# Chunked attention heads run on across tiles: one slot of other work per score group, an own bank for the short group, moves by half tiles

## The chip, the cores and the metric

One core of one Trainium2 chip runs the whole program. The metric is device time in microseconds (us) of one execution; lower is better. A profile of one execution gives the times of single instructions.

## The reference

A residual block over 4096 positions of width 1024, with two parallel groups. `h = rms_norm(x)` and `proj = h @ w_in` give a pooling mixer (value, gate) and eight attention heads of width 64 (q, k, v, gate). Each chunk of 64 positions attends to itself and the eight chunks before it:

```python
s = einsum('bqhd,bkhd->bhqk', qb, kb) * scale + bias      # clipped relative positions
s = where(valid, s, MASK_VALUE)
p = softmax(s, axis=-1)
y_attn = einsum('bhqk,bkhd->bqhd', p, vb) * silu(attn_g)
x = x + concatenate([y_pool, y_attn]) @ w_out
return rms_norm(x, final_norm_gain)
```

## The kernel before

Every operand of a matmul is split into a high and a low fp16 part, and the input projection is a seven-product scheme on blocks. The program has three phases, each written as one list of instructions for each engine, with semaphores between them; the order written out is the order in which each engine works.

**First phase** (`h_phase_*`): 16 pairs of 128-row blocks are normalised, split and stored in `h_dram`, with the value and gate columns. x comes through two buffers, one load ahead. At pair 5 SP (the engine that issues the transfers) sends the relative-bias rows, written out per query and per key for all heads, from DRAM to DRAM. **Second phase** (`q_phase_*`): the pooling branch and its half of the output projection, whose sum goes to `r_dram`.

**Third phase** (`a_phase_*`): 16 tiles of 256 queries. For each of eight heads TensorE issues:
- `maxima` (two, for the two blocks of 128 queries): scores by query in the double bank `wide`; VectorE's `maximum` adds the bias and takes the row maximum. They run two heads ahead.
- `max_rows`: the maxima as a row in bank `tra`; ScalarE's `max_row` copies it into the query operand, so that the next scores come out with the maximum taken off. One head ahead.
- `scores`: up to three groups of columns by key (512, 512 and 256), turn by turn in the two banks `sta[n % 2]`; VectorE's `add_bias` works on the second; ScalarE's `exponential` writes `p32` (two buffers) and rounds it to `p_h`; GpSimd's `p_lo` makes the low part.
- `values`, one head behind: both parts with V, into `pva`; VectorE's `attend` normalises and gates into `y`.

Between them stand pieces of other work: the key and query projection of the next tile (`kq_half`, 14 products in 28 halves; products take turns in `bankx` and `banky`, with `kq_take` on VectorE and copies on ScalarE; `kq_hi` and `kq_lo` round the finished operand), and the output projection of an earlier tile (`output`, four parts in two halves, `residual` on VectorE). `KQ_SLOTS` says how many halves each head takes; heads 6 and 7 take halves of the output instead.

Between two tiles stands `boundary(t)`: the rest of the output of tile t-2, the last head's `values`, the transposes of `y` (`branch_transposes`, in `tra` and `wide`, rounded by `branch_hi` and `branch_lo`), and the first two heads' maxima with eight product halves among them. The new keys and queries go by twelve transfers within SBUF (`move_k`, `move_q`, 128 KB each) to their operand places, sent once the tile before has all its scores. Then follow V (`load_v`), the gates, the residual, and seven loads of the projection's operand two tiles on (`load_hop3`), all on SP's one queue.

Of the kernel before, what the change touches and what calls it, by code (L numbers as in the profile page):

```python
# [20 lines left out]
P = 128  # L21
# [78 lines left out]
def build(nc, x, norm_gain, w_in, pool_w, pool_scale, rel_fwd, rel_rev, w_out, final_gain, out):  # L100
# [13 lines left out]
    with ctx:  # L114
# [3 lines left out]
        def sem(name):  # L118
# [21 lines left out]
        Z = sb("stages", [P, 38400 // 4], F32)  # L140
# [60 lines left out]
        p32 = view(Z, 18432, (2, 512), F32)  # L201
# [6 lines left out]
        names = """ident0 ident_ready id16 consts log_ready inv_ready ones_ready gain_loaded pw_loaded small_loaded  # L208
# [3 lines left out]
            ext_done ext_stored bias_stored over""".split()  # L212
# [280 lines left out]
        def h_phase_dve(dve):  # L493
# [120 lines left out]
            def bias_rows():  # L614
# [3 lines left out]
                nc.vector.tensor_copy(ident16[:, :], ident[:, :]).then_inc(H["id16"], 1)  # L618
# [166 lines left out]
        def h_phase_sp(sp):  # L785
# [33 lines left out]

            load_x(0)  # L820
# [24 lines left out]
            for p in range(1, PAIRS):  # L845
# [25 lines left out]
        names = """psc_done over mm p1_done u_done c11_done tanh_done z_done step_done y_done yh_done yl_done op_mm r_done  # L871
# [384 lines left out]
        def q_phase_pool(pool):  # L1256
# [30 lines left out]
            pool.wait_ge(H["bias_stored"], 32)  # L1287
# [9 lines left out]
        def q_phase_sp(sp):  # L1297
# [58 lines left out]
            load_gate(sp, 0)  # L1356
            load_bias(sp)
            move_k(sp, 0)
            for s in range(PRODUCTS):
                load_hop3(sp, 1, s)  # L1360
            for b in range(PBLK):
                n = PBLK * (PTILES - 1) + b
                store_res(n)
                if b < 2:
                    load_res(n + 2)
                if b == 1:
                    move_q(sp, 0)
            for s in range(2):
                sp.wait_ge(r_stored[s], 16 * 2 * PTILES)
            sp.nop().then_inc(Q["over"], 1)  # L1370

        names = """moved_k moved_q kq_mm kq_p kq_u nat_hi nat_lo v_loaded gate_loaded k_ones mask_rows bias_q_loaded
# [5 lines left out]
        hop3_loaded = [sem(f"a_hop3_loaded{s}") for s in range(PRODUCTS)]  # L1378
        res_loaded = [sem(f"a_res_loaded{s}") for s in range(2)]
# [46 lines left out]

        KQ_PRODUCT = (0, 1, 2, 3, 4, 6, 5)
        KQ_TAKES = {1: 0, 2: 1, 3: 2, 5: 3, 6: 4}


        KQ_BEFORE = 8
        KQ_SLOTS = ((2, 2), (2, 1), (2, 1), (2, 1), (2, 1), (2, 2), (0, 0), (0, 0))
        K_HI_AT, Q_HI_AT = (2, 0), (6, 0)

        def slot(h, i):

# [711 lines left out]
```

## Time and profile before

| | before |
|---|---|
| time, median of 3 runs | 1805.46 us (1803.0 to 1809.53) |
| time of the profiled execution | 1807.35 us |
| its span, first to last instruction | 1805.6 us |
| TensorE busy | 1644.2 us (91%) |
| VectorE busy | 1068.5 us (59%) |
| ScalarE busy | 843.5 us (47%) |
| GpSimd busy | 708.4 us (39%) |
| mean granted TensorE clock | 0.984 |

The busy time of an engine is the union of its instructions' times. TensorE's matmuls overlap one another, so that its busy time is no measure of how fast it could go. Idle time of an engine is put down to the instruction that it waited for.

### The profile page before, as it was taken

The numbers are of one execution on the slowest core, as the hardware profiler recorded it, in microseconds if no ns is written. First come the engines' busy times: TensorE is split into PE (matmuls) and PEld (weight loads), VectorE is DVE, ScalarE is ACT, GpSimd is POOL, SyncE is SP. The second block draws the span as 40 slices with busy tenths as digits, with TensorE's granted clock in tenths as the row PEclk, the third lists the DMA queues.
The fourth block names the chain that finished last, engine by engine and source line by source line (L and its number), as shares of the span: only waits on it lengthen the run. The fifth ranks groups of instructions, "written<-read, shape, count | busy, mean of one in ns | idle before, by whom it ended". The sixth has DMA issues, their size and how long they took to land. (4 is left out here: it accounts for less than half of the span.)

```text
span 1805.6 us, 43913 instructions
## 1 busy us (share of the span) xinstructions
PE 1644.2 (91%) x17920; PEld 1220.5 (68%) x17920; DVE 1068.5 (59%) x2188; ACT 843.5 (47%) x1580; POOL 708.4 (39%) x734
## 2 busy tenths in 40 slices
PE   5999699999999999999879999999999999999977
PEld 2554345568667676777567787778777787778854
DVE  7767477747456556544355565556655565556654
ACT  5554455422112111111145766567565765667565
POOL 3534345311112121001324644465545654456544
PEclk8999899999999999999989999999999999999999
DMA  5655574462542453244743342442334332442332
GB/s 205 209 204 200 196 247 170 170 251 72 186 164 83 163 187 129 83 159 166 218 147 101 99 131 79 136 131 106 102 106 148 112 125 72 136 148 90 107 94 83
DMA packets 111231, 257.84 MB, mean 143 GB/s; under 512 B 11928, under 2 KB 24744, under 8 KB 108984
## 3 DMA queue, kind: packets, MB, share of 16 engines
q1 hardware_dynamic: 109992, 253.73, 42.0%
q8 instruction: 143, 2.34, 0.5%
q0 software_dynamic: 1040, 1.31, 0.4%
q14 instruction: 56, 0.46, 0.1%
HBM read 151.33 MB, written 83.48 MB: 130 GB/s over the span
## 5 line engine op out<-in xcount | busy, mean ns | idle before, releaser
L2029 POOL TENSOR_TENSOR stages<-stages 128x512 f16<-128x512 f32 (+1 forms) x368 | 379.3, 1046 | 445.3 <-ACT stages L1814 445.1
L1489 PE MATMUL bank<-middle,weights 128*128 128x128 f16 x1792 | 315.0, 220 | 14.0 <-DVE middle L1526 13.1
L1492 PE MATMUL bank<-middle,weights 128*128 128x128 f16 x1792 | 314.6, 220 | 0.0
L1491 PE MATMUL bank<-middle,weights 128*128 128x128 f16 x1792 | 314.5, 220 | 0.0
L1808 ACT ACTIVATE stages<-bank,log_ps 128x512 f32<-128x512 f32 (+1 forms) x368 | 222.0, 603 | 163.9 <-POOL stages L2029 93.4
L1899 DVE CUSTOM_DVE_ANT_0 stages<-bank,stages 128x640 bf16<-128x640 f32 (+4 forms) x256 | 200.0, 781 | 158.2 <-PE bank L1647 157.9
L975 PE MATMUL bank<-middle 128*128 128x256 f16 x784 | 215.7, 275 | 7.5 <-DVE stages L1103 7.5
L977 PE MATMUL bank<-middle 128*128 128x256 f16 x784 | 215.7, 275 | 0.0
L978 PE MATMUL bank<-middle 128*128 128x256 f16 x784 | 215.6, 275 | 0.0
L1677 PE MATMUL bank<-middle 128*128 128x128 f16 (+1 forms) x840 | 169.4, 244 | 46.5 <-ACT stages L1808 41.9
L1814 ACT ACTIVATE stages<-stages 128x512 f16<-128x512 f32 (+1 forms) x368 | 203.5, 553 | 11.7
L288 PE MATMUL bank<-weights,middle 128*128 128x512 f16 x448 | 172.5, 385 | 25.9 <-DVE stages L584 15.9
L1489 PEld LDWEIGHTS bank<-middle,weights 128*128 128x128 f16 x1792 | 175.9, 98 | 17.5 <-DVE middle L1526 15.9
L1623 PE MATMUL bank<-entry,stages 128*128 128x512 f16 x768 | 181.1, 379 | 1.6 <-DVE stages L1876 1.0
L998 PE MATMUL bank<-entry,stages 128*128 128x512 f16 x768 | 171.6, 380 | 11.4 <-DVE entry L1195 11.4
L1491 PEld LDWEIGHTS bank<-middle,weights 128*128 128x128 f16 x1792 | 176.1, 98 | 0.4
L1492 PEld LDWEIGHTS bank<-middle,weights 128*128 128x128 f16 x1792 | 175.8, 98 | 0.0
L290 PE MATMUL bank<-weights,middle 128*128 128x512 f16 x448 | 172.2, 384 | 0.0
L291 PE MATMUL bank<-weights,middle 128*128 128x512 f16 x448 | 171.9, 384 | 0.0
L1262 POOL TENSOR_TENSOR stages<-stages 128x512 f16<-128x512 f32 x32 | 39.4, 1230 | 282.1 <-ACT stages L1051 282.1
L998 PEld LDWEIGHTS bank<-entry,stages 128*128 128x128 f16 x768 | 74.3, 98 | 101.2 <-DVE entry L1195 17.3
L1680 PE MATMUL bank<-middle 65*128 65x256 f16 x616 | 130.3, 242 | 0.0
(147 smaller groups left out, 3544.3 us busy)
## 6 DMA issues: line engine op xcount, KB each, us to landing
entry<-in_x SPq DMA_DIRECT2D x64, 512.0 KB, 3.6
h_ops<-middle SPq DMA_DIRECT2D x16, 1792.0 KB, 6.1
middle<-h_ops SPq DMA_DIRECT2D x112, 256.0 KB, 5.1
middle<-h_ops SPq DMA_DIRECT2D x49, 512.0 KB, 6.9
middle<-middle SPq DMA_DIRECT2D x192, 128.0 KB, 2.3
residual<-entry SPq DMA_DIRECT2D x32, 512.0 KB, 2.8
entry<-residual SPq DMA_DIRECT2D x30, 512.0 KB, 4.1
out<-entry SPq DMA_DIRECT2D x30, 512.0 KB, 2.9
```

The lines of the kernel that those rows point to most:

```text
L975: nc.tensor.matmul(bank, wh, hop[:, :, s, 0, kt, :], start=(kt == 0 and s < 4), stop=False, skip_group_check=True)
L977: nc.tensor.matmul(bank, wh, hop[:, :, s, 1, kt, :], start=False, stop=False, skip_group_check=True)
L978: mm = nc.tensor.matmul(bank, wl, hop[:, :, s, 0, kt, :], start=False, stop=(kt == 3), skip_group_check=True)
L998: mm = nc.tensor.matmul(op[n2], part, w[:, kt, n2 * 512:(n2 + 1) * 512], start=(kt == 0 and w is wot_h and part is yh), stop=(kt == NKT - ...
L1489: nc.tensor.matmul(dst, wh, hop3[:, o, 0, kt, :], start=(kt == 0 and s < 2 and pair == 0), stop=False, skip_group_check=True)
L1491: nc.tensor.matmul(dst, wh, hop3[:, o, 1, kt, :], start=False, stop=False, skip_group_check=True)
L1492: mm = nc.tensor.matmul(dst, wl, hop3[:, o, 0, kt, :], start=False, stop=(kt == 3), skip_group_check=True)
L1623: mm = nc.tensor.matmul(bank[:, :], yh, w, start=(m == 0), stop=(m == 11))
L1808: nc.scalar.activation(p32[:, s, a:b], sta[s][:, a:b], ACT.Exp, bias=log_ps[:, 0:1]).then_inc(A["exp_done"], 1)
L1814: nc.scalar.activation(p_h[:, h % 2, c + a:c + b], p32[:, s, a:b], ACT.Copy).then_inc(A["ph_done"], 1)
L1899: nc.vector.tensor_tensor_reduce(junk2[:, c:640], wide[:, c:640], bias_q[:, h, c:640], 1.0, -3e38, ALU.add, ALU.max, m16[:, h % 2, j:j + 1 ...
L2029: nc.gpsimd.tensor_tensor(p_l[:, h % 2, c + a:c + b], p32[:, s, a:b], p_h[:, h % 2, c + a:c + b], ALU.subtract).then_inc(A["pl_done"], 1)
```

## The change

The part between tiles is gone. `ahead(t, h, n)` counts heads across tiles, so maxima and row maxima of the next tile are issued in the last heads of this one, and the last head's values in the first head of the next. Each head has three slots (`SLOTS`), one behind each score group; slots 0 to 13 take one whole product each, slots 15 to 22 one half of the output of the tile before; slots 14 and 23 are empty. The products' banks alternate over both operands. Each score group has its own bank and its own `p32` buffer; the short one lies in the second half of `pva` and waits until the head before is normalised. The transposes go in two rounds of four, by halves of the heads, at the ends of the first two heads of the next tile, both in `tra`. Keys, queries and gates are moved by halves of the heads, the first half while the tile before still works on its second. In the last tile the output of the tile before stands in slots 7 to 14, and the first halves of its own output in slots 17 to 20. In the first phase the bias rows are sent in four parts, two heads at each of the pairs 5 to 8. Some semaphores that nobody waits for are gone.

```diff
...
-p32 = view(Z, 18432, (2, 512), F32)
+p32 = [view(Z, 18432, (512,), F32), view(Z, 20480, (512,), F32), view(Z, 38144, (2 * P,), F32)]
...
+    def store_bias(h):
+        if h == 0:
+            sp.wait_ge(H["ext_stored"], 16)
+        for r, (dst, width) in enumerate(((bq_dram, 640), (bk_dram, 256))):
+            sp.dma_start(dst[h:h + 2], bass.AP(rel_dram.tensor, (r * HEADS + h) * EXT + P - 1,
+                                       [[EXT, 2], [-1, P], [1, width]])).then_inc(H["bias_stored"], 16)
...
-        if p == BIAS_AT + 2:
-            sp.wait_ge(H["ext_stored"], 16)
-            for r, (dst, width) in enumerate(((bq_dram, 640), (bk_dram, 256))):
-                sp.dma_start(dst, bass.AP(rel_dram.tensor, r * HEADS * EXT + P - 1,
-                                          [[EXT, HEADS], [-1, P], [1, width]])).then_inc(H["bias_stored"], 16)
+        if 0 <= p - BIAS_AT - 2 < HEADS // 2:
+            store_bias(2 * (p - BIAS_AT - 2))
...
+SLOTS = 3
+K_HI_HEAD, Q_HI_HEAD = 2, 4
+HALF = HEADS // 2
+def kq_slot(t, h, a):
+    x = SLOTS * h + a
+    return divmod(x, PRODUCTS) if t < LAST and x < 2 * PRODUCTS else None
+def output_slot(t, h, a):
+    x = SLOTS * h + a
     if t == LAST:
-        return ((t - 1, h - 4, i),) if h >= 4 else ()
-    return ((t - 1, h - 6, i),) if t > 0 and h >= 6 else ()
+        if 7 <= x < 15:
+            return t - 1, (x - 7) // 2, (x - 7) % 2
+        return (t, x - 17, 0) if 17 <= x < 21 else None
+    return (t - 1, (x - 15) // 2, (x - 15) % 2) if t > 0 and 15 <= x < 23 else None
+def round_at(t, h):
+    if t > 0 and h < 2:
+        return t - 1, h
+    return (t, 0) if t == LAST and h == HALF else None
+def squares_at(t, h):
+    if t == LAST:
+        return {3: ((t - 1, 0),), 5: ((t - 1, 1),)}.get(h, ())
+    return {6: ((t - 1, 0),), 7: ((t - 1, 1),)}.get(h, ()) if t > 0 else ()
+def finish_at(t, h):
+    found = ((t - 2, 1),) if t > 1 and h == 0 else ()
+    if t == LAST:
+        return {4: ((t - 1, 0),), 6: ((t - 1, 1),)}.get(h, found)
+    return ((t - 1, 0),) if t > 0 and h == 7 else found
...
-def kq_bank(s):
-    bank = (bankx, banky, bankx, banky, bankx, banky, bankx)[s]
+def kq_bank(w, s):
+    bank = (bankx, banky)[(w + s) % 2]
     at = (0, 0, AT, AT, 0, AT, AT)[s]
     return bank[:, at:at + AT]
...
-    dst = kq_bank(s)[:, pair * P:(pair + 1) * P]
+    dst = kq_bank(w, s)[:, pair * P:(pair + 1) * P]
...
-def load_gate(sp, t):
-    at_least(sp, A["ya_done"], 2 * HEADS * t)
+def load_gate(sp, t, half):
+    at_least(sp, A["ya_done"], 2 * HEADS * t if half else 2 * HEADS * t - 2 * HALF)
+    cols = slice(half * AT, (half + 1) * AT)
     for j in range(2):
-        sp.dma_start(gate[:, j, :], z_dram[2 * t + j]).then_inc(A["gate_loaded"], 16)
+        sp.dma_start(gate[:, j, cols], z_dram[2 * t + j, :, cols]).then_inc(gate_loaded[half], 16)
...
+def scored(t, half):
+    return seq(t - 1, HEADS if half else HALF, 0)
+def move_q(sp, t, half):
     sp.wait_ge(A["nat_lo"], 2 * t + 2)
     if t > 0:
-        sp.wait_ge(A["st_mm"], seq(t - 1, HEADS, 0))
+        sp.wait_ge(A["st_mm"], scored(t, half))
+    h2 = slice(2 * half, 2 * half + 2)
     for o in range(2):
-        half = slice(o * DH, (o + 1) * DH)
-        move(sp, qs[0:DH, o, :, :], nat[half, 1, 0, :, :], "moved_q")
-        move(sp, qs[DH:P, o, :, :], nat[half, 1, 1, :, :], "moved_q")
-        move(sp, qm[0:DH, o, :, :], nat[half, 1, 0, :, :], "moved_q")
...
+def before(t, h, g):
+    at, head = (t, h - 1) if h > 0 else (t - 1, HEADS - 1)
+    if at < 0:
+        return 0
+    have = [x for x, _ in groups(at)]
+    return seq(at, head, have.index(g)) + 1 if g in have else 0
...
+def score_bank(g):
+    return (sta[0][:, :], sta[1][:, :], pva[:, 2 * P:4 * P])[g]
...
+def out_bank(t, i):
+    if t == LAST:
+        return (bankx[:, :], banky[:, :], wide[:, 0:512], wide[:, 512:1024])[i]
+    return (bankx[:, :], banky[:, :])[i % 2]
...
+            if t == LAST and i >= 2:
+                pe.wait_ge(A["max_done"], 2 * HEADS * ATILES)
+            else:
+                at_least(pe, A["out_done"], 4 * t + i - 1)
             if i < 2 and t < LAST:
                 pe.wait_ge(A["kq_u"], 5 * min(2 * t + 6, 2 * ATILES))
+        elif t == LAST:
+            pe.wait_ge(A["ytl_done"], 2 * t + 2)
         for m in range(6 * half, 6 * half + 6):
             kt, p = m // 3, m % 3
             yh = (yT_l if p == 2 else yT_h)[:, kt, j * P:(j + 1) * P]
             w = (wob_l if p == 1 else wob_h)[:, kt, n2 * 512:(n2 + 1) * 512]
-            mm = nc.tensor.matmul(bank[:, :], yh, w, start=(m == 0), stop=(m == 11))
+            mm = nc.tensor.matmul(out_bank(t, i), yh, w, start=(m == 0), stop=(m == 11))
         if half == 1:
...
         n = 2 * HEADS * t + 2 * h + j
         if n > 0:
             pe.wait_ge(A["max_done"], n)
...
+        if h >= 2 and round_at(t, h - 2):
+            of, r = round_at(t, h - 2)
+            pe.wait_ge(A["ytl_done"], 2 * of + r + 1)
         for j in range(2):
             mm = nc.tensor.matmul(tra[:, j * P:(j + 1) * P], m16[:, h % 2, j:j + 1].to_broadcast([P, P]),
                                   ident16[:, :], start=True, stop=True)
...
             pe.wait_ge(A["mrow_done"], HEADS * t + h + 1)
+        if g == 2:
...
+    def branch_transposes(t, r, rows):
+        pe.wait_ge(A["ya_done"], 2 * (HEADS * t + HALF * (r + 1)))
+        pe.wait_ge(A["mrow_done"], rows)
+        for q in range(4):
+            kt = 2 * r + q // 2
+            mm = nc.tensor.transpose(tra[:, q * P:(q + 1) * P], y[:, q % 2, kt * P:(kt + 1) * P], ident[:, :])
         mm.then_inc(A["yt_mm"], 1)
...
+    def other(t, h, a):
+        if kq_slot(t, h, a):
+            x = SLOTS * h + a
+            kq_half(pe, t + 1, 2 * x)
+            kq_half(pe, t + 1, 2 * x + 1)
+        if output_slot(t, h, a):
+            output(*output_slot(t, h, a))
+    def head(t, h):
+        scores(t, h, 0)
+        other(t, h, 0)
+        t2, h2 = ahead(t, h, 2)
+        if t2 < ATILES:
+            maxima(t2, h2, 0)
+        scores(t, h, 1)
+        t1, h1 = ahead(t, h, 1)
+        if t1 < ATILES:
+            max_rows(t1, h1)
+        other(t, h, 1)
+        if t > 0 or h > 0:
+            values(*ahead(t, h, -1))
+        if t2 < ATILES:
+            maxima(t2, h2, 1)
+        other(t, h, 2)
+        scores(t, h, 2)
+        if round_at(t, h):
+            of, r = round_at(t, h)
+            branch_transposes(of, r, HEADS * t + h + 2)
+    for j in range(2):
+        maxima(0, 0, j)
+    max_rows(0, 0)
+    for j in range(2):
+        maxima(0, 1, j)
+    for t in range(ATILES):
         for h in range(HEADS):
-            last = len(groups(t)) - 1
-            for k in range(2):
-                if k < last or (k == 0 and last == 0):
-                    scores(t, h, k)
-                if t < LAST:
-                    for x in slot(h, k):
-                        kq_half(pe, t + 1, x)
-                for at, i, half in output_slot(t, h, k):
-                    output(at, i, half)
-                if k == 0 and h + 1 < HEADS:
-                    max_rows(t, h + 1)
-                if h + 2 < HEADS:
-                    maxima(t, h + 2, k)
-            if last > 0:
-                scores(t, h, last)
-            if h > 0:
-                values(t, h - 1)
-    for t in range(ATILES):
-        boundary(t)
-        heads(t)
+            head(t, h)
     values(LAST, HEADS - 1)
-    for j in range(2):
-        branch_transposes(LAST, j)
+    branch_transposes(LAST, 1, HEADS * ATILES)
...
         if n == 0:
             act.wait_ge(Q["op_mm"], PBLK * PTILES)
...
+    def head(t, h):
+        exponential(t, h, 0)
+        other(t, h, 0)
+        exponential(t, h, 1)
+        t1, h1 = ahead(t, h, 1)
+        if t1 < ATILES:
+            max_row(t1, h1)
+        other(t, h, 1)
+        if t < LAST and h == K_HI_HEAD:
+            kq_hi(act, 2 * t + 2)
+        other(t, h, 2)
+        exponential(t, h, 2)
+        if t < LAST and h == Q_HI_HEAD:
+            kq_hi(act, 2 * t + 3)
+        if round_at(t, h):
+            branch_hi(*round_at(t, h))
+        for of, j in squares_at(t, h):
+            square(of, j)
+        if t == 0 and h < NKT:
+            wob_hi(h)
+    max_row(0, 0)
...
+    def branch_lo(t, r):
+        dve.wait_ge(A["yth_done"], 2 * t + r + 1)
         nc.vector.scalar_tensor_tensor(
-            out=yT_l[:, :, j * P:(j + 1) * P], in0=bank[:, 0:512].rearrange("p (k n) -> p k n", k=NKT),
...
+    def other(t, h, a):
+        if kq_slot(t, h, a):
+            w, s = kq_slot(t, h, a)
+            if s in KQ_TAKES:
+                kq_take(dve, 2 * t + 2 + w, KQ_TAKES[s])
+        if output_slot(t, h, a):
+            of, i, half = output_slot(t, h, a)
+            if half == 1:
+                residual(of, i)
+    def head(t, h):
+        other(t, h, 0)
+        t0, h0 = ahead(t, h, -1)
+        if t0 >= 0 and round_at(t0, h0):
+            branch_lo(*round_at(t0, h0))
+        t2, h2 = ahead(t, h, 2)
+        if t2 < ATILES:
+            maximum(t2, h2, 0)
+        add_bias(t, h)
+        other(t, h, 1)
+        if t > 0 or h > 0:
+            attend(t0, h0)
+        if t2 < ATILES:
+            maximum(t2, h2, 1)
+        other(t, h, 2)
+        for of, j in finish_at(t, h):
+            finish(of, j)
+        if t == 0 and h < NKT:
+            wob_lo(h)
...
@@ -2041,16 +2069,17 @@
     for t in range(ATILES):
         for h in range(HEADS):
-            p_lo(t, h)
-            if t > 1 and h in (1, 2):
-                rstd(t - 2, h - 1)
-            if t < LAST and h == K_HI_AT[0]:
-                kq_lo(pool, 2 * t + 2)
-            if t < LAST and h == Q_HI_AT[0]:
+            for k, (g, _) in enumerate(groups(t)):
+                p_lo(t, h, k)
+                if k == 0:
+                    for of, j in finish_at(t, h):
+                        rstd(of, j)
+                if g == BIASED and t < LAST and h == K_HI_HEAD:
...
-            load_gate(sp, t)
+            load_gate(sp, t, 1)
...
-            for j in range(2):
-                store(t - 2, j)
         if t > 0:
             for j in range(2):
                 load_residual(t - 1, j)
-        if t + 2 < ATILES:
-            for s in range(PRODUCTS):
-                load_hop3(sp, t + 2, s)
+        if t < LAST:
+            move_k(sp, t + 1, 0)
+            if t + 2 < ATILES:
+                for s in range(PRODUCTS):
+                    load_hop3(sp, t + 2, s)
+            load_gate(sp, t + 1, 0)
+            move_q(sp, t + 1, 0)
...
```

## Rows read from the trace of the kernel before

**Rows 1.** Windows, thirteen tiles: busy us and (instructions) per engine, clock, DMA share, GB/s
```profile
984.00:1734.00 750.00, 690.56 (x10714) 587.44 (x10713) 439.26 (x1066) 479.33 (x884) 401.15 (x390) 1.00 0.37 114
```

**Rows 2.** Waits of TensorE, 984 to 1734: total us, times, longest
```profile
PE bank L1677 <- ACT stages L1808: 37.4, 65, 1.3
PE bank L1489 <- DVE middle L1526: 10.5, 13, 0.8
PE bank L1647 <- DMA middle<-middle: 8.4, 10, 1.3
```

**Rows 3.** Timeline of TensorE in one head: start us, length us
```profile
1183.22 0.22 PE L1677 MATMUL bank<-middle 128*128 128x128 f16 x1
...
1183.67 0.22 PE L1489 MATMUL bank<-middle,weights 128*128 128x128 f16 x1
...
1184.34 0.44 PE L1647 MATMUL bank<-middle 128*128 128x128 f16 x4
1184.62 0.27 PE L1677 MATMUL bank<-middle 128*128 128x256 f16 x1
...
1184.84 0.19 PE L1705 MATMUL bank<-middle,stages 128*128 128x65 f16 x1
...
1185.71 0.19 PE L1707 MATMUL bank<-middle,stages 128*128 128x65 f16 x1
```

**Rows 4.** Timeline of three engines around the bias rows, 164 to 197
```profile
166.31 7.04 SPq L867 DMA_DIRECT2D bias_by_key<-rel_rows  x1
...
190.29 1.06 ACT L335 ACTIVATE entry<-entry 128x1024 bf16<-128x1024 f32 x1 [22.54 <-DMA entry<-in_x]
...
196.76 0.59 PE L288 MATMUL bank<-weights,middle 128*128 128x512 f16 x1 [15.87 <-DVE stages L584]
```

**Rows 5.** Lines of three engines, 1214 to 1445: busy us, mean ns, idle before
```profile
L1899 DVE CUSTOM_DVE_ANT_0 stages<-bank,stages 128x640 bf16<-128x640 f32 x64 | 52.7, 823 | 40.9 <-PE bank L1647 40.8
L1913 DVE TENSOR_TENSOR bank<-bank,stages 128x512 f32<-128x512 f32 x32 | 22.2, 695 | 17.0 <-PE bank L1680 17.0
L1526 DVE SCALAR_TENSOR_TENSOR middle<-bank,middle 128x256 f32<-128x256 f32 x40 | 16.9, 422 | 7.0 <-PE bank L1492 5.7 <-issue 1.2
L1931 DVE SCALAR_TENSOR_TENSOR middle<-bank,rc,middle 128x64 f32<-128x64 f32 x64 | 15.2, 280 | 1.1
...
L1924 DVE RECIPROCAL rc<-bank 128x2 f32<-128x2 f32 x32 | 5.4, 170 | 8.0 <-PE bank L1707 7.9
L1876 DVE SCALAR_TENSOR_TENSOR stages<-bank,stages 128x512 f16<-128x512 f32 x8 | 5.2, 686 | 1.5 <-ACT stages L1784 1.5
...
L1808 ACT ACTIVATE stages<-bank,log_ps 128x512 f32<-128x512 f32 x64 | 43.8, 685 | 25.7 <-POOL stages L2029 11.3 <-PE bank L1680 7.9 <-DVE bank L1913 5.9
L1814 ACT ACTIVATE stages<-stages 128x512 f16<-128x512 f32 x64 | 40.4, 632 | 2.0
...
L1534 ACT ACTIVATE middle<-middle 128x1024 f16<-128x1024 f32 x8 | 8.5, 1059 | 0.2
...
L1538 POOL TENSOR_TENSOR middle<-middle 128x1024 f16<-128x1024 f32 x8 | 17.1, 2133 | 0.0
```

**Rows 6.** Timeline of SP's issues, then DMA issues of the run (KB, us to landing)
```profile
1249.78 5.94 SPq L1557 DMA_DIRECT2D middle<-h_ops  x7
1265.68 8.04 SPq L1584 DMA_DIRECT2D middle<-middle  x12
...
entry<-in_x SPq DMA_DIRECT2D x64, 512.0 KB, 3.6
...
middle<-middle SPq DMA_DIRECT2D x192, 128.0 KB, 2.3
...
middle<-values SPq DMA_DIRECT2D x32, 258.0 KB, 3.0
```

**Rows 7.** Timeline of TensorE at the end of the last tile
```profile
1785.22 1.09 PE L1719 MATMUL bank<-ident,middle 128*128 128x128 f32 x8 [0.78 <-DVE middle L1931]
...
1793.00 5.34 PE L1623 MATMUL bank<-entry,stages 128*128 128x512 f16 x24 [0.35 <-DVE middle L1943]
```

More of the change, by code:

```diff
@@ L1532, in kq_hi @@
             act.wait_ge(A["kq_u"], 5 * w + 5)
-            at_least(act, A["moved_q" if w % 2 else "moved_k"], 96 * (w // 2))
+            for half in range(2):
+                at_least(act, (moved_q if w % 2 else moved_k)[half], 96 * (w // 2))
             nc.scalar.activation(nat_of(w, 0), cs_flat(), ACT.Copy).then_inc(A["nat_hi"], 1)
@@ L1722, in boundary @@
-            def boundary(t):
-                def steps(first, last):
-                    if t < LAST:
-                        for x in range(first, last):
-                            kq_half(pe, t + 1, x)
-                if t > 1:
-                    output(t - 2, 2, 0)
-                    output(t - 2, 2, 1)
-                if t > 0:
-                    values(t - 1, HEADS - 1)
-                if t > 1:
-                    output(t - 2, 3, 0)
-                    output(t - 2, 3, 1)
-                if t > 0:
-                    for j in range(2):
-                        branch_transposes(t - 1, j)
-                steps(0, 2)
-                maxima(t, 0, 0)
-                steps(2, 4)
-                maxima(t, 0, 1)
-                steps(4, 6)
-                max_rows(t, 0)
-                maxima(t, 1, 0)
-                steps(6, 8)
-                maxima(t, 1, 1)
@@ L1866, in a_phase_act @@
+            max_row(0, 0)
+            for t in range(ATILES):
+                for h in range(HEADS):
+                    head(t, h)
+            branch_hi(LAST, 1)
             for j in range(2):
-                branch_hi(LAST, j)
-            for t in (LAST - 1, LAST):
-                for j in range(2):
-                    square(t, j)
+                square(LAST, j)
         def a_phase_dve(dve):
-            def branch_lo(t, j):
-                bank = tra if j == 0 else wide
-                dve.wait_ge(A["yth_done"], 2 * t + j + 1)
+            def branch_lo(t, r):
+                dve.wait_ge(A["yth_done"], 2 * t + r + 1)
@@ L1903, in add_bias @@
             def add_bias(t, h):
-                k = [g for g, have in groups(t)].index(BIASED)
+                k, _ = group_of(t, BIASED)
                 n = seq(t, h, k)
-                bank = sta[n % 2]
+                bank = score_bank(BIASED)
                 dve.wait_ge(A["st_mm"], n + 1)
@@ L1987, in heads @@
-            def heads(t):
-                for h in range(HEADS):
-                    for k in range(2):
-                        if k == (0 if t == 0 else 1):
-                            add_bias(t, h)
-                        if h + 2 < HEADS:
-                            maximum(t, h + 2, k)
-                        if t < LAST:
-                            for w, s in kq_steps(slot(h, k)):
-                                if s in KQ_TAKES:
-                                    kq_take(dve, 2 * t + 2 + w, KQ_TAKES[s])
-                        for at, i, half in output_slot(t, h, k):
-                            if half == 1:
-                                residual(at, i)
-                    if h > 0:
-                        attend(t, h - 1)
-                    if t > 1 and h in (2, 3):
-                        finish(t - 2, h - 2)
-                    if t == 0 and h < NKT:
-                        wob_lo(h)
@@ L2008, in a_phase_dve, with other @@
-            for t in range(ATILES):
-                boundary(t)
-                heads(t)
+            def other(t, h, a):
+                if kq_slot(t, h, a):
+                    w, s = kq_slot(t, h, a)
+                    if s in KQ_TAKES:
[23 more added lines that the diff above has]
+                    wob_lo(h)
@@ L2011, in a_phase_dve @@
+            mask_bias()
+            for h in range(2):
+                for j in range(2):
+                    maximum(0, h, j)
+            for t in range(ATILES):
+                for h in range(HEADS):
+                    head(t, h)
             attend(LAST, HEADS - 1)
-            for j in range(2):
-                branch_lo(LAST, j)
-            for j in range(2):
-                finish(LAST - 1, j)
+            branch_lo(LAST, 1)
             for i in range(4):
```

249 lines of the change are left out of this document (91 added, 158 removed).

## The prediction

> **What bounds the kernel now.** The chain that ended last covers only the final 16 us, so I took the windows by stage first, then TensorE's waits, then its timeline for one head, and the other engines' durations last. The reader sees in [rows 1] that from 984 to 1734 us, thirteen tiles of 57.7 us, TensorE is busy 690.6 of 750 us while VectorE, ScalarE and GpSimd have 59, 64 and 53%: it does the work, and its stops are what can be won. [Rows 2] name the stops in that stretch: short score groups and bank turns (L1677 behind ScalarE's exponentials, 37.4 us in 65 stops), the first product after the boundary (L1489, 10.5 in 13), and the moved keys and queries (L1647, 8.4 in 10). With two small kinds beside them this is 58 us in some 92 stops. A stop costs more than its idle time: a 128x128 matmul lasts 0.22 us but the next starts 0.056 later (twelve in 0.67) [rows 3], so 0.165 us of overlap is lost too. (58 + 92 x 0.165)/13 = **5.6 us lost a tile**, 52.1 us of work.
>
> Outside the tiles one stop stands out: SP spends 7 us issuing the bias rows, the block of x behind them lands at 190.29, ScalarE has waited 22.5 us for it and TensorE 15.9 [rows 4].
>
> **The steady tile after the change.** Per head TensorE issues, by [rows 3]: two large score groups 0.45 each, the short one 0.22, maxima 0.28 twice, rows 0.11 (two of 0.056), values 0.89, and a slot is 24 matmuls, 1.34 (an output half, six of 512 columns, about the same). A consumer starts some 0.2 after the issue ends (0.22 of the last matmul less its 0.056, plus a hand-over of 0.04). With three slots the new order is, in us from the head's start: group 0 to 0.45, slot 1.79, maxima 2.07, group 1 2.52, rows 2.63, slot 3.97, values 4.86, maxima 5.14, slot 6.48, short group 6.70. Durations below are those of [rows 5].
>
> *What goes.* Score banks are now reused a whole head later, so ScalarE's exponential (0.69) is long over: the 65 stops go. The product after the boundary uses the other bank than the last one, so its stop goes. The boundary's bare run of vector maxima goes, and the maxima that open a tile are issued in heads 6 and 7 of the tile before.
>
> *What comes.* (a) The short group shares a bank with the values' accumulator and waits for VectorE's normalising: values end 4.86, +0.20, reciprocal 0.17+0.04, two of 0.28 overlapping to 0.48, +0.06 to resume = 5.81. A slot covers that, except in heads 4 and 7, where slot 2 is empty: 5.81-5.14 = 0.67 each, **1.3**. (b) The transposes use the row bank; in heads 1 and 2 `max_rows` must wait for `branch_lo`, which on VectorE stands behind the first slot's `kq_take`: 1.79 + 0.20 + 0.36 (0.42, the next starts a little earlier) + 0.69 + 0.06 = 3.10 against 2.52, **0.6 each, 1.2**. Behind it on VectorE stand a maximum and `add_bias`: exponential 1 then starts near 4.5, its copy ends 5.9 and the row copy 6.3, before the next head asks at 7.3. So nothing further. (c) The query half. The last take ends at 4.6 in head 4. ScalarE has exponential and copy of the late short group to 7.0, `kq_hi` 1.06 to 8.1, GpSimd 2.13 to 10.3. SP then issues six half moves. Twelve whole ones went out in 8.04, 0.64 apart, landing 2.3 after issue [rows 6]. Halves have the same 64 rows of half the bytes: between 0.33 and 0.64 apart, I take 0.55, as I cannot see that fewer bytes shorten the issue; last landing 10.3+2.8+2.3 = 15.4. TensorE asks for them in head 6: head 4 takes 6.0, head 5 6.6, then 1.8 = 14.4. **1.0**, bounds 0 and 1.5. Head 1's `load_v` stands behind twelve half moves (6.6 to 7.7 after the tile's last scores), +0.5 for the second, +3.0 to land: 10.1 to 11.2, against 11.7 when values ask: hidden, by little.
>
> Everything else that is moved has cover: the K operand's `kq_lo` in head 2 delays the short group's low part to 3.2 into head 3, asked for at 3.97; the two squares and finishes lie in VectorE's and ScalarE's free third; SP's queue holds 24 moves, 7 loads of `hop3` and the rest, some 24 of 55 us, and the seven loads go before `move_q(t+1, 0)`, done by head 5. Gate halves (loads of 128 rows) have half a tile. The new buffer, semaphores and removed nops are nothing on any engine's time.
>
> Sum 1.3+1.2+1.0 = 3.5 against 5.6: 2.1 a tile, **27 us over thirteen**. Per-tile loss may be 2 to 5.5.
>
> **First two tiles.** They end today at 984 [rows 1]; the new order is walked through from about 891. The prologue has no products between the first maxima (short ones, of 128 and 256 columns), about 2 us. Tile 0's heads have one score group of three blocks and short values, 4.9 us with their slots and 3.6 for head 4: head 5 starts near 916. But tile 1's first maxima now stand in head 6, asked for near 919, and `move_q` waits on SP for `wob`'s roundings, the key half, seven `hop3` loads (5.9 us for seven in [rows 6]) and the path of (c): landing near 929. A stop of 10 us; heads 6 and 7, one after the other down the serial loop, take 6.4; tile 1 has some 45 us of work (fewer blocks) and 3.5 of stops: 985. **-1**, bounds -6 and +5.
>
> **Last tile**, now from 1734 [rows 1] to the span's end at 1805.6: 71.7 us. A head without slots follows one loop: maxima issued 0.73, +0.2, maximum 0.83, bias 0.70, exponential and copy 1.26 (0.69 and 0.63, overlapping a little), row copy 0.4 (an estimate, fewer columns than the 0.63), hand-overs: 4.2 us. Heads in order, with slots of output and transposes (four of 0.11 [rows 7]): 4.6, 5.4, 5.8, 6.6, 7.0, 4.9, 6.0, 40.3 in all. Head 7 has values at 5.7-6.6, transposes done at 8.0, both roundings to 9.4, four second halves 5.2 to 14.6, and 7.3 from the last matmul (ends 1798.34) to the end of the span [rows 7]: 21.9. But here heads 0 and 1 are short: `values` of head 1 is asked at 6.4 while V lands at 8.9 to 10.9: 3 more. 65.2: **6.5 won**, bounds 2 and 10.
>
> **The bias rows in four parts.** All the rows kept x away until 190.29, 24.0 us after 166.31 [rows 4]. With a load's own landing L, a quarter delays it by (24.0-L)/4; L is 3.6 by the page's median [rows 6], and more beside other stores, say 5.3. The flood's delay D = 24-L cost TensorE 15.9, so D-15.9 was hidden: 4.5 or 2.8. Each part then costs 5.1-4.5 = 0.6 or 4.7-2.8 = 1.9; four of them 2 to 8, I take 5. **11 won**, bounds 8 and 16.
>
> **Sum.** 27 - 1 + 6.5 + 11 = 44 us. The profiled execution took 1807.35 us with a span of 1805.6; its sum is 1763, and the median of the three runs, 1805.46, lies 1.9 under it: **1761**.
>
> *A rule against the change.* The moves go from 128 KB to 64 KB, twice as many, on one queue; [rows 6] have 0.64 between issues of the whole ones. The Trainium skill (DMA: Bandwidth & Descriptors, "Rules for kernel authors") says to merge many small transfers, since below 64 KB one pays mostly overhead. By that rule a half costs what a whole does, and the sum loses 0.5 us a tile, 7 in all. No row here shows a half move.
>
> **Rivals.**
> Likeliest, 0.50: as above, 1745 to 1777.
> Waits nearly all hidden, 0.16: halves land in time, the empty-slot stops stay: 2.0 lost a tile, bias parts free, V in time: 1734. For it: idle engines. Against: (a) and (b) have no cover in the order.
> The query half late by 2 us more, 0.15: SP or the seven loads hold it; 26 us back: 1787. For it: all of (c) is serial over four engines and a queue. Against: the loads are two heads earlier.
> The stops move but stay, 0.10: each head pays ScalarE's and GpSimd's serial path as today (5.3 lost a tile): 1784. Against: every bank and buffer has a head's distance.
> Slower, 0.05: the same place (c), half moves costing more each than whole ones. The gain of 44 is gone at 3.4 us a tile, that is six moves at 0.55+0.57 = 1.1 us apart; at 1.3 it is about 1820. For it: nothing shown of halves; against: a whole one needs 0.64.
> No change within 0.3%, 0.04: bias parts gain nothing because each lands on x, and the tiles gain half.
>
> Range 1738 to 1788, holding the likeliest case and most of the second and third. Faster by over 0.3% (5.4 us, about what this measurement tells from no change) 0.91, within 0.04, slower 0.05.
>
> **What would show it.** Tiles of 55.6 us; no L1677-like stop behind ScalarE; `max_rows` idle 0.4 behind `branch_lo` twice a tile; the short group idle 0.5 behind VectorE in heads 4 and 7; maxima of head 6 waiting for a move about 1; a 10 us wait near 920; no 15.9 us stop near 197 but small ones in four pairs. The prediction falls if half moves are slow, if GpSimd's low parts come late for `values`, or if the clock drops in the longer stop of tile 0.

## The result, and the profile after

The changed kernel takes 1860.15 us (median of 4 runs, 1857.59 to 1867.6) where the kernel before, run beside it, takes 1806.38 (1803.0 to 1809.53): 1.0305 times as long, 95% interval 1.027 to 1.034. Forecast was 1761. The profiled execution took 1860.0 us with a span of 1858.2, 52.6 more than before's 1805.6. Two executions of the experiments below, one in e8 (2051.75 us) and one in e11 (1804.7 us), ran at a lower granted clock than the others of their kernels (0.792 and 0.936), and the ratios leave them out.

The windows come first: the first four stages of the changed kernel (start and end, length, then busy us and instructions of TensorE, its weight loads, VectorE, ScalarE, GpSimd, then clock, DMA share, GB/s).

```profile
0.00:435.20 435.20, 346.95 (x1697) 175.41 (x1698) 266.06 (x327) 189.90 (x330) 163.34 (x200) 0.92 0.51 182
435.20:936.80 501.60, 483.90 (x3793) 356.70 (x3791) 271.14 (x542) 85.28 (x196) 82.22 (x73) 0.99 0.43 148
936.80:1044.30 107.50, 81.80 (x1174) 71.24 (x1173) 56.13 (x175) 49.34 (x99) 33.16 (x37) 0.87 0.37 114
1044.30:1785.10 740.80, 684.94 (x10706) 587.41 (x10704) 427.63 (x1067) 475.23 (x884) 387.43 (x391) 1.00 0.38 115
```

The clock is 0.92 in the first phase, and TensorE idles 88 of 435 us there. With the timeline's marks (the first product of the second phase, the heads at which tiles 2 and 15 begin) the stages compare so:

| stage | before | after | difference | forecast |
|---|---|---|---|---|
| up to the second phase | 384.4 | 435.2 | +50.8 | -11 |
| second phase's products | 504.7 | 501.6 | -3.1 | 0 |
| from there to the end of tile 1 | 94.9 | 107.5 | +12.6 | +1 |
| thirteen tiles | 750.0 | 740.8 | -9.2 | -27 |
| last tile, to the end | 71.6 | 73.1 | +1.5 | -6.5 |

The sign of the result is made in the first phase, where the bias rows go out; but the attention did not win what it was to win either: 57.0 us a tile, not 55.6.

TensorE's waits in the first stage (total, times, longest), where [rows 4] had one stop of 15.87:

```profile
PE bank L288 <- DVE stages L584: 44.9, 3, 15.3
...
PE bank L240 <- ACT stages L403: 15.6, 2, 14.4
```

All of TensorE's stops in this stage sum to 88.2 us, before to 45.4: 43 of the 50.8. That the clock is at half for 71.7 us of it, before for 23.9, is the likely source of most of the rest.

Each part holds the loads as the whole did. SyncE's timeline around the first two of the four parts (start us, us):

```profile
165.63 1.12 SPq L825 DMA_DIRECT2D bias_by_query<-rel_rows  x1
166.82 6.37 SPq L825 DMA_DIRECT2D bias_by_key<-rel_rows  x1
173.23 9.58 SPq L788 DMA_DIRECT2D entry<-in_x  x1
...
202.40 1.12 SPq L825 DMA_DIRECT2D bias_by_query<-rel_rows  x1
203.57 2.75 SPq L825 DMA_DIRECT2D bias_by_key<-rel_rows  x1
206.37 13.88 SPq L788 DMA_DIRECT2D entry<-in_x  x1
```

The x block behind the first part lands at 190.41; before, behind the whole, at 190.26. The DMA view says why: busy tenths of the 16 engines and GB/s, in 40 slices. This is the kernel before, 164 to 192:

```profile
DMA  9977994554545554555555555555559999999999
GB/s 471 512 328 328 378 283 128 190 190 179 195 179 194 187 201 197 205 201 205 205 205 205 205 205 216 191 195 193 195 215 354 287 392 433 385 379 377 333 335 318
```

and this the changed one, 166 to 192:

```profile
DMA  9888411111111111111111111178879999995898
GB/s 397 353 353 299 130 39 39 51 47 55 51 51 47 51 55 47 55 47 55 47 55 55 47 55 47 50 85 106 124 280 345 408 405 367 321 348 178 241 351 251
```

The whole, eight heads, keeps about half of the engines busy (5 tenths) at some 200 GB/s; a part of two heads keeps an eighth busy (1 tenth) at some 50. A quarter of the bytes at a quarter of the rate takes as long: a part's 256 packets of 2560 bytes take from 169.4 to 182.5, the whole's 1024 from 168.5 to 182.8. A single such packet takes 0.11 us in both; the part has 2.0 of them under way at a time, the whole 7.6. The engines in use follow the outermost count of the access, which is the heads. The Trainium skill (DMA: Bandwidth & Descriptors, "Why a DMA increments its semaphore by 16 and not by 1") says that a DMA issued so runs on the largest number of engines up to 16 that divides the slowest dimension; by it 8 and 2, as the trace has it.

In the thirteen tiles, TensorE's waits in 1044.4 to 1785.2 (against [rows 2]; a tenth behind the tiles' marks, so that each stop between two tiles counts once):

```profile
PE bank L1713 <- issue: 18.8, 13, 2.5
PE bank L1746 <- DVE middle L1975: 15.3, 26, 0.6
PE bank L1726 <- DVE stages L1921: 12.7, 26, 0.7
PE bank L1774 <- issue: 8.9, 12, 1.2
```

The stops behind ScalarE's exponentials are gone, as forecast. The second row is (a) of the prediction, the third (b), the first (c): maxima that wait for moved queries ("issue", since the profile shows no releaser; they start as the last move lands). The fourth, `values` behind V, was held to be hidden. SyncE's queue in one tile, first half of the keys, seven loads, gates, first half of the queries:

```profile
1245.02 3.68 SPq L1639 DMA_DIRECT2D middle<-middle  x6
1248.74 4.31 SPq L1589 DMA_DIRECT2D middle<-h_ops  x7
1253.09 0.90 SPq L1604 DMA_DIRECT2D middle<-gates  x2
1255.22 3.67 SPq L1628 DMA_DIRECT2D middle<-middle  x6
```

Six half moves take 3.67 us, which is 0.64 apart, as whole ones were [rows 6]. The last lands at 1260.39, and the maxima start at 1260.48, after an idle of 1.08.

### The profile page after: what moved, and what is told of

Same layout as the page of the kernel before. It is cut to its first block and busy times, and to the rows that moved or that the text cites. A ratio compares the mean times of both kernels' runs of the same rounds, so it can differ in the third digit from the quotient of the medians.

```text
span 1858.2 us, 44337 instructions
## 1 busy us (share of the span) xinstructions
PE 1649.0 (89%) x17920; PEld 1224.9 (66%) x17920; DVE 1058.1 (57%) x2188; ACT 837.8 (45%) x1580; POOL 696.3 (37%) x734
## 5 line engine op out<-in xcount | busy, mean ns | idle before, releaser
L2057 POOL TENSOR_TENSOR stages<-stages 128x512 f16<-128x512 f32 (+1 forms) x368 | 366.5, 1000 | 450.7 <-ACT stages L1864 450.6
L288 PE MATMUL bank<-weights,middle 128*128 128x512 f16 x448 | 175.4, 391 | 55.1 <-DVE stages L584 44.9
L1691 PE MATMUL bank<-entry,stages 128*128 128x512 f16 x768 | 190.0, 385 | 1.4 <-DVE stages L1921 1.4
L1746 PE MATMUL bank<-middle 128*128 128x128 f16 (+1 forms) x840 | 164.3, 243 | 19.8 <-DVE middle L1975 18.3
L1003 PE MATMUL bank<-entry,stages 128*128 128x512 f16 x768 | 171.3, 380 | 11.1 <-DVE entry L1200 11.1
L290 PE MATMUL bank<-weights,middle 128*128 128x512 f16 x448 | 174.8, 390 | 0.0
L291 PE MATMUL bank<-weights,middle 128*128 128x512 f16 x448 | 174.4, 389 | 0.0
L1713 PE MATMUL bank<-middle 128*128 128x128 f16 (+1 forms) x848 | 109.7, 244 | 40.1 <-issue 21.7
L1267 POOL TENSOR_TENSOR stages<-stages 128x512 f16<-128x512 f32 x32 | 39.3, 1229 | 281.7 <-ACT stages L1056 281.7
L1557 DVE SCALAR_TENSOR_TENSOR middle<-bank,middle 128x256 f32<-128x256 f32 x160 | 67.9, 424 | 134.4 <-PE bank L1527 134.4
```

What stands on the lines that cost most here:

```text
L1691: mm = nc.tensor.matmul(out_bank(t, i), yh, w, start=(m == 0), stop=(m == 11))
L1746: nc.tensor.matmul(dst, keys(ks, slice(0, P), h, r), queries(qs, slice(0, P), h, qcols), start=True, stop=False)
L2057: nc.gpsimd.tensor_tensor(p_l[:, h % 2, c + a:c + b], p32[g][:, a:b], p_h[:, h % 2, c + a:c + b], ALU.subtract).then_inc(A["pl_done"], 1)
```

## The experiments

**Which part made it slow.** Two kernels exchange the bias parts: the changed kernel with the rows whole, the kernel before with them in four.

```diff
-if 0 <= p - BIAS_AT - 2 < HEADS // 2:
-    store_bias(2 * (p - BIAS_AT - 2))
+if p == BIAS_AT + 2:
+    sp.wait_ge(H["ext_stored"], 16)
+    for r, (dst, width) in enumerate(((bq_dram, 640), (bk_dram, 256))):
+        sp.dma_start(dst, bass.AP(rel_dram.tensor, r * HEADS * EXT + P - 1,
+                                  [[EXT, HEADS], [-1, P], [1, width]])).then_inc(H["bias_stored"], 16)
...
```

> The changed kernel with the bias rows sent whole at pair 5, as before the change. Theory A (the loss lies in the first phase: a part of the bias rows holds the queue as long as the whole did): the four stops of about 15 us in the first phase become one, some 46 us less than the changed kernel, 1812 us, so 3 to 6 us above the kernel before. Theory B (the loss lies in the attention order): no more than 5 us less, 1855 us.

Measured: 1809.64 us (median of 10, 1806.47 to 1818.4) beside 1807.1 of before, ratio 1.002 (1.0004 to 1.0036). One stop of 15.5 us is back in place of 60.5 in five.

The other way round, the same edit reversed in the kernel before:

> The kernel before with only the bias rows changed: four parts of two heads at pairs 5 to 8. Theory A: the first phase has four stops of 14 to 16 us in place of one, 1806 + 46 = 1852 us. Theory B: 1795 to 1803 us, as predicted for parts that each cost a quarter.

Measured: 1856.87 us, ratio 1.0279 (1.0257 to 1.0302). Its waits show the changed kernel's stops without its attention:

```profile
PE bank L288 <- DVE stages L584: 44.7, 3, 15.2
...
PE bank L240 <- ACT stages L403: 13.1, 1, 13.1
```

So the parts cost some 50 us in either kernel, and the attention's new order, alone, gains nothing.

**Is it the number of parts or their shape?** Again four parts, but each of 32 rows of all eight heads:

```diff
-sp.dma_start(dst[h:h + 2], bass.AP(rel_dram.tensor, (r * HEADS + h) * EXT + P - 1,
-             [[EXT, 2], [-1, P], [1, width]]))
+sp.dma_start(dst[:, 16 * h:16 * h + 32, :], bass.AP(rel_dram.tensor,
+             r * HEADS * EXT + P - 1 - 16 * h, [[EXT, HEADS], [-1, 32], [1, width]]))
```

> The changed kernel, but each of the four parts holds 32 rows of all eight heads in place of all rows of two heads: the same bytes, 256 packets of each width. Theory A1 (a transfer is spread over as many DMA engines as its outermost count allows: 8 for eight heads, 2 for two heads; the Trainium skill, DMA: Bandwidth & Descriptors, 'Why a DMA increments its semaphore by 16 and not by 1', says the largest count up to 16 that divides it): each part takes a quarter of the whole, stops of 0 to 2 us in place of 15, 1858 - 59 + 0 to 8 = 1799 to 1807 us. Rival A2 (any DRAM-to-DRAM part ahead of the load of x costs about 15 us, however it is shaped): 1858 us.

Measured: 1808.98 us (median of 10, 1802.49 to 1818.96), ratio 1.0016 (0.9996 to 1.0035), on the changed kernel. SyncE's timeline for the first part and the load behind it:

```profile
165.34 1.29 SPq L825 DMA_DIRECT2D bias_by_query<-rel_rows  x1
166.68 1.25 SPq L825 DMA_DIRECT2D bias_by_key<-rel_rows  x1
167.97 0.57 SPq L788 DMA_DIRECT2D entry<-in_x  x1
```

SyncE issues the x load in 0.57 us, not 9.58. The 256 packets of 2560 bytes of each of the four parts, again 0.11 to 0.12 us each, have 6.0 to 7.7 under way at a time and take 3.5 to 4.8 us, where the parts of two heads, 2.0 at a time, took 13.0 to 14.1. The two kinds of stop are down:

```profile
PE bank L288 <- DVE stages L584: 5.2, 3, 2.5
PE bank L240 <- ACT stages L403: 2.9, 2, 1.9
```

The same edit in the kernel before:

> The kernel before with the bias rows in four parts of 32 rows of all heads at pairs 5 to 8, and nothing else of the change. Theory A1: the one stop of 15.9 us goes and stops of 0 to 2 us come in four pairs: 1806 - 16 + 0 to 8 = 1790 to 1798 us. Rival A2: 1852 us.

Measured: 1802.06 us (1799.1 to 1822.75, median of 10), ratio 0.9987 (0.9961 to 1.0013), not told from no change. The second phase starts at 377.4 there and 378.5 in the changed kernel, against 384.4: the parts, so shaped, win 6 to 7 us of the 11 forecast, where one profiled run of this same phase differs from another by up to 4 (376.5 to 380.4 in e3 and the runs built on it). That e1 and e3 do not differ in their medians shows how little of this a time of the whole kernel tells. All that follows is built on e3, called the base.

**Why does the attention gain so little?** One edit each. First V, loaded ahead of the second half of the queries:

```diff
 move_k(sp, t, 1)
+load_v(sp, t)
 move_q(sp, t, 1)
-load_v(sp, t)
```

> On top of the changed kernel with bias parts by rows (1809 us): on SP's queue the loads of V stand ahead of the six half moves of the queries' second half. Theory C (V comes late only because twelve half moves, 0.64 us apart, are issued ahead of it): the stop before the values of head 1 (0.9 us a tile with its restart, 3.8 in the last tile) goes, 1809 - 11 - 2 = 1796 us. Rival: V is late by its landing, or the stop moves to the maxima of head 4, whose queries now come later: 1809 us.

Measured: 1789.28 us (1785.73 to 1796.44), ratio 0.9893 (0.9866 to 0.9921), 20 less than the base. The stop is gone and no other has grown; V lands 8.5 us after the tile's start in the median, not 12.4, and tiles take 56.0 us, not 57.2. In the profiled runs the thirteen tiles are 15.7 us shorter and the last tile 4.1, together 19.8, as the medians have it; up to tile 2 this run is 6.3 longer than the base's, so that the spans (1801.5 and 1787.9) differ by 13.6 only. Of the 19.8, V's stops make 9.0 us in 12 stops, 9.0 + 12 x 0.165 = 11.0, and 4.1 in the last tile. The clock is at half for 10.2 us of the base's thirteen tiles and for 3.4 of these, which by an estimate from these lengths is up to 3.4 us more. The rest, some 1 us, stays open.

Next the seven loads of `hop3` behind the first half of the queries:

```diff
 move_k(sp, t + 1, 0)
-if t + 2 < ATILES:
-    for s in range(PRODUCTS):
-        load_hop3(sp, t + 2, s)
 load_gate(sp, t + 1, 0)
 move_q(sp, t + 1, 0)
+if t + 2 < ATILES:
+    for s in range(PRODUCTS):
+        load_hop3(sp, t + 2, s)
```

> On top of the changed kernel with bias parts by rows (1809 us): the seven loads of the projection's operand stand behind the first half of the queries on SP's queue, not ahead of it. Theory D (in tile 0 the queries stand behind these loads; in later tiles they only land some 0.5 us later beside them): the stop of 11 us in tile 0 becomes 6 to 7, and each later tile's stop at the maxima of head 6 is 0.3 to 0.6 shorter, 1809 - 4 - 6 = 1799 us. Rival: nothing but GpSimd's rounding decides when the queries go, 1809 us.

Measured: 1794.03 us (1792.04 to 1795.31), ratio 0.9914 (0.9896 to 0.9931), 15 less than the base. Tile 0's stop falls from 10.3 to 7.3 us, tiles from 57.2 to 56.7. The query stops sum to 14.1 us instead of 18.6.

Then the queries' rounding ahead of the short group's exponential on ScalarE and of its low part on GpSimd:

```diff
 if t < LAST and h == K_HI_HEAD: kq_hi(act, 2 * t + 2)
+if t < LAST and h == Q_HI_HEAD: kq_hi(act, 2 * t + 3)
 other(t, h, 2)
 exponential(t, h, 2)
-if t < LAST and h == Q_HI_HEAD: kq_hi(act, 2 * t + 3)
...
```

> On top of the changed kernel with bias parts by rows (1809 us): ScalarE rounds the queries ahead of the short group's exponential of head 4, and GpSimd makes their low part ahead of that group's low part, as both do for the keys in head 2. Theory E (the path of the queries is serial over ScalarE, GpSimd and six issues): queries go 1.2 to 1.4 us earlier, the stop at the maxima of head 6 falls from 1.8 us a tile with its restart to 0.5, 1809 - 17 = 1792 us. Rival F (SP is still busy with the seven loads and the gates until then): 0 to 3 us.

Measured: 1804.31 us (1796.28 to 1816.54, median of 10), ratio 0.9977 (0.9952 to 1.0001): little, and nothing in the profiled tiles (57.4 us). Its timeline and DMA issues of one tile say where the gain went:

```profile
1254.77 3.68 SPq L1640 DMA_DIRECT2D middle<-middle  x6
1258.49 3.45 SPq L1590 DMA_DIRECT2D middle<-h_ops  x7
1261.99 1.07 SPq L1605 DMA_DIRECT2D middle<-gates  x2
1263.40 4.04 SPq L1629 DMA_DIRECT2D middle<-middle  x6
```
```profile
middle<-middle SPq DMA_DIRECT2D x6, 64.0 KB, 3.0
```

From the keys' start to the queries' start it is now 8.6 us, not 10.2 as in the changed kernel and the base, but the moves then run beside the seven loads, which land up to 1267.74, and need 3.0 us to land in the median, where the same six of the base in such a tile need 2.5. Over tiles 2 to 13 the queries are issued 39.3 us after the tile's start in the median, not 40.3, a single move needs 3.5 us to land, not 2.6, and the last one lands at 46.0 in both: earlier issue is paid back by later landing. That fits e6 too, which takes the loads out of the queries' way (2.0 us to land).

Last `branch_lo` ahead of the first slot's work on VectorE:

```diff
 def head(t, h):
-    other(t, h, 0)
     t0, h0 = ahead(t, h, -1)
     if t0 >= 0 and round_at(t0, h0): branch_lo(*round_at(t0, h0))
+    other(t, h, 0)
```

> On top of the changed kernel with bias parts by rows (1809 us): on VectorE the low part of the transposes stands ahead of the first slot's product in the head, not behind it. Theory G (max_rows waits for it only because of that order; ScalarE's part is done 1.2 us into the head): both stops of 0.64 us a tile go, 1809 - 17 = 1792 us. Rival: the transposes' path as a whole is late, 1806 to 1809 us.

Measured: 1804.76 us (median of 10, nine between 1795.41 and 1808.62, one at 2051.75), ratio 0.9969 (0.9948 to 0.999). Its waits in the thirteen tiles:

```profile
PE bank L1775 <- issue: 19.6, 11, 3.7
PE bank L1714 <- issue: 18.4, 13, 2.0
PE bank L1747 <- DVE middle L1976: 15.3, 26, 0.6
PE bank L1775 <- POOL stages L2058: 5.8, 2, 3.0
```

All 26 stops at `max_rows` (12.6 us) are gone, but those at the values of head 1 have grown from 9.0 us in 12 to 25.4 in 13 (the last row stands at the same place in its tiles, so it is counted with the first). V lands 13.0 us after the tile's start in the median, in the base 12.4: it comes when the queue brings it, and TensorE only reaches that wait sooner. The tiles take 57.2 us in both.

**Together.** If the edits hide one another, their sum must show once V and the loads are out of the way. First the two of SyncE's order:

> The changed kernel with the bias rows in four parts by rows, and two edits of SyncE's order: the V loads ahead of the second half of the query moves, and the seven operand loads for the tile after next behind the first half of the query moves. Alone, the one gave 1789 us and the other 1794, where the kernel with neither gave 1809. Theory: they act at different places, the one on the stop of 0.6 to 1.3 us at the values of each tile, the other on the stop at the maxima of tile 0 (10.4 to 7.5 us) and on what follows it, so their gains add: 1809 - 19.6 - 15 = 1775 us, with no stop left at the values. Rival: what both relieve is the same queue, and the stop at the maxima that waits for the queries (1.1 to 1.2 us a tile) takes the place of what goes: 1784 us and above.

Measured: 1779.31 us (three between 1777.36 and 1780.72, one at 1804.7), ratio 0.984 (0.9809 to 0.987): the gains nearly add. The waits of the thirteen tiles, 55.6 us each:

```profile
PE bank L1747 <- DVE middle L1976: 15.3, 26, 0.6
PE bank L1714 <- issue: 13.8, 13, 1.9
PE bank L1727 <- DVE stages L1922: 12.5, 26, 0.5
```

Then all four:

> The two edits of SyncE's order, and with them the early rounding of the queries and branch_lo ahead of the other work on VectorE, which alone gave 3 to 4 us each. Theory: branch_lo first took 0.64 us out of two heads of each tile, but where V comes at a time set by the queue the stop at the values grew by as much (1.1 us became 2.2 and 3.1 in two of the tiles). With V early that cover is gone, so 13 x 1.28 = 17 us come through, and the early rounding offers another 13 x 0.5 = 6: 1775 - 23 = 1752 us. Rival: the tile's length is now set by the chain of the queries (products, rounding, six moves, landing), so the stop at the maxima grows by the 1.28 us that goes at the max_rows: 1770 us and above.

Measured: **1745.74 us** (1740.99 to 1750.1), ratio 0.9649 (0.9617 to 0.9681), 32 to 34 less than with two (without and with e11's longest execution), though the two added ones gave some 4 each alone. Window and waits of the thirteen tiles:

```profile
984.20:1676.40 692.20, 675.36 (x10707) 586.68 (x10705) 429.19 (x1067) 477.06 (x884) 388.08 (x391) 1.00 0.40 123
```
```profile
PE bank L1747 <- DVE middle L1976: 15.3, 26, 0.6
PE bank L1714 <- issue: 1.5, 2, 0.9
```

A tile takes 53.2 us. The stops account for the gain: 41.6 us in 65 have become 16.8 in 28, with the overlap of 0.165 each 30.9 us, and the thirteen tiles are 30.6 shorter. Of it 12.5 are the stops behind `branch_lo` and 12.3 those for the queries; what each of the two edits gives behind the first two was not run. What is left is (a) of the prediction, the short group behind VectorE. The rival (the queries' chain sets the tile) falls: its stops went from 13.8 to 1.5 us. The six moves, with the loads behind them, land in 2.0 us in the median.

Last, the output one slot earlier, so that the empty slot of head 4 is filled:

```diff
-return (t - 1, (x - 15) // 2, (x - 15) % 2) if t > 0 and 15 <= x < 23 else None
+return (t - 1, (x - 14) // 2, (x - 14) % 2) if t > 0 and 14 <= x < 22 else None
```

> The same four edits, and the first half of the output products one slot earlier, in the third slot of the fifth head, which is empty in the changed kernel. Theory: the short group's scores of that head wait 0.75 us for VectorE's attend since nothing fills the slot; with it filled, one of the two such waits of a tile goes: 14 x 0.7 = 10 us less than without it, 1742 us. Rival: the output product's bank is that of the last query product, which VectorE takes only in the slot before; TensorE then waits there 0.5 to 1 us for VectorE instead, and the time is the same as without the edit, within 4 us.

Measured: 1747.78 us (1745.41 to 1749.67), ratio 0.9668 (0.9642 to 0.9694): no gain, but not by the rival's mechanism. The waits have no stop at the output's bank; they have two new ones a tile at the scores (thirteen tiles):

```profile
PE bank L1747 <- ACT middle L1842: 10.7, 13, 0.8
PE bank L1747 <- ACT stages L1859: 10.2, 13, 0.8
```

Both stops behind VectorE's normalising went, and ScalarE, with the row copy and an exponential, is late by 0.8 twice instead; tiles take 53.5 us. Both new stops stand at the tile's end, at the short group of head 7 and at the first group of the head behind it. With the output one slot earlier, slots 22 and 23, both of head 7, are empty. That this leaves the head too short for ScalarE's work is the likely reason; it was not tried by itself.

## Why the prediction was wrong

**The failed step: "The bias rows in four parts".** It took the delay of a load to shrink with the bytes ("a quarter delays it by (24.0-L)/4") and won 11 us. It measured +50.8 in the stage, the whole of the sign: the parts in the kernel before cost 50 (e2), whole rows in the changed kernel take them away (e1), and four parts that keep all eight heads outermost win 6 to 7 (e3, e4). The rate of a transfer was taken as given, when the edit changed it fourfold. The two rows that should have raised the question lay in the trace of before: its DMA view shows the flood at half of the engines, at 200 GB/s, with eight heads outermost. The rivals had the parts free or gaining nothing; none had them cost anything. Four stops of some 15 us stand where one was, and with each go 13.7 to 17.1 us at half of the clock (186.3 to 200.0 is the first).

**"The steady tile", 2.1 us won a tile.** Right in kind: the stops behind ScalarE went, and (a), (b), (c) came where they were said to. (a) measured 0.75 twice a tile for 0.67, and (b) 0.65 for 0.6 (15.3/26 and 12.7/26, each with the overlap of 0.165). The mis-sized term is (c), 1.0 forecast: 18.8/13 + 0.165 = 1.6. Half moves are 0.64 apart, not 0.55, 0.5 us over six, and behind the seven loads they land late in some tiles. What the Trainium skill (DMA: Bandwidth & Descriptors, "Rules for kernel authors") was quoted for, that a half costs what a whole does, the trace bears out for the issue (0.64 us). V, "hidden, by little", is not: with the larger interval, and 4.6 us for the second six moves, it costs 8.9 us in 12 stops, (8.9 + 12 x 0.165)/13 = 0.8 a tile. The four kinds make (55.7 + 77 x 0.165)/13 = 5.3 lost a tile, where 3.5 was forecast and before loses 5.6. The tile is 0.7 shorter; some 0.3 of that the waits don't account for. The rival "the stops move but stay" gave 5.3, the very figure, by luck: it put the stops on each head's path over ScalarE and GpSimd, behind which none was left.

**"First two tiles", 1 us lost.** Measured 12.6. The stop was forecast at 10 and is 10.8; what is missing is around it. TensorE idles seven times more for 0.5 to 2.1 us, five times before that stop and twice behind it, mostly behind VectorE's row maxima: 8.7 us, where the prediction allowed 2 for the prologue. And the clock is at half (1.2 of 2.4 GHz) from 974.8 to 995.3, 11.3 us of it behind the stop, which by an estimate from that length costs up to 5.7. The prediction named the clock as a risk and gave it no price.

**"Last tile", 6.5 won.** Measured 1.5 lost. V's stop is 3.8 us with the overlap, for 3. Behind it come seven smaller ones of 0.5 to 1.8, and fourteen of the output's last matmuls run at half of the clock, 0.43 us apart instead of 0.216: 3 us.

**The range.** It reached no further than 1788 because the bias term was held within 8 and 16 us (its own parts, four of 0.6 to 1.9, give 8 to 13.5). Without that step (e1) the changed kernel takes 1810, still above the range: every term of the attention came out worse than forecast.

**What the attention's order is worth.** On its own, nothing to be measured (e1: 1.002, e3 against e4: 0.4% more). With the order of the queue and of three engines matched to it, 692.2 us for the thirteen tiles instead of 750: e9 is 62.5 us below before (1808.23 beside it) and 114 below the changed kernel. The forecast of 27 us over thirteen tiles was too high for the change as it stood and too low for what its order allows. Which parts of the change e9 needs was not tried.

## What to carry to other kernels

Before a transfer is cut up, read in the DMA view how many engines the whole keeps busy, and cut along a dimension that leaves the outermost count as it is. When an edit that removes a stop gives nothing, look at the next wait set by a time and not by work (here V at the end of a queue), and test the edits together: singly two of four gave 4 us each, behind the other two some 33. On one queue, put first what is asked for first (V, e5), and large loads behind small urgent moves (e6), since here they delayed the moves after issue too.

## What the runs showed of the hardware

- Packets of 2560 bytes from DRAM to DRAM take 0.10 to 0.12 us each whether the transfer's outermost count is 8 or 2. With 8 up to 7.7 are under way at a time, some 200 GB/s; with 2 it is 2.0, some 50 GB/s (before, after, e3).
- SBUF moves of 64 rows go out 0.64 us apart with 64 KB as with 128 KB [rows 6]; the landing differs by 0.3 us (medians of the runs after and before: 2.0 and 2.3).
- Six such moves issued right behind seven loads of 256 KB land in 3.5 us in the median over tiles 2 to 13 (e7), started some 1 us later in 2.6 (e3), with the loads behind them in 2.0 (e6, e9).
- With each of four stops of some 15 us in the first phase the granted clock goes to 0.5 for 13.7 to 17.1 us.
